# First weight unit in single k-tiles, a unit rounded ahead of the row scales, and two DVE instructions moved

## What is computed

```python
def rms_norm(x, g):
    y = x32 * lax.rsqrt(jnp.mean(x32 * x32, axis=-1, keepdims=True) + RMS_EPS)
    return (y * g).astype(x.dtype)

# layer 0: mla_stick_breaking_mixer (8 MLA heads, 8 stick-breaking heads), then swiglu
proj = u @ w_in            # u = rms_norm(x, g), 256 x 1024 by 1024 x 2208
h = h + (jax.nn.silu(u @ w_gate) * (u @ w_up)) @ w_down
# layer 1: chunk_band_mixer (16 heads, softmax over a band, p @ v, then w_out), then swiglu
s = softmax(q k^T * scale + bias); o = s @ v; h = h + o @ w_out
# last block: three attention branches (blocks, dilated, sliding window with a sink)
branches = [o_a * silu(ga), o_b * silu(gb), o_c * silu(gc)]
merged = sum(sigmoid(gate_logits) * (branches @ w_branch)); x = x + merged @ w_out
```

## Time and profile before

| | us |
|---|---|
| median of 3 runs | 980.27 (979.02 to 981.82) |
| the profiled execution | 978.15 |
| its span, first to last instruction | 976.4 |
| PE busy | 968.8 (99%), 4936 matmuls |
| DVE busy | 623.1 (64%) |
| ACT busy | 593.0 (61%) |
| POOL busy | 17.1 (2%) |

### The profile page before, as it was taken

How to read it: one execution, slowest core, us unless ns; L and a number is a source line. 1 busy time by engine, 2 the same in 40 slices (tenths; PEclk the granted TensorE clock), 3 DMA queues, 4 the chain that set the end, 5 groups by cost and what they waited for, 6 DMA issues and landing times.

```text
span 976.4 us, 13095 instructions
## 1 busy us (share of the span) xinstructions
PE 968.8 (99%) x4936; PEld 796.5 (82%) x4936; DVE 623.1 (64%) x765; ACT 593.0 (61%) x918; POOL 17.1 (2%) x30
## 2 busy tenths in 40 slices
PE   9999999999999999999999999999999999999998
PEld 7888788888888877788888888887878888788887
DVE  5776775555556767565555555867676667786654
ACT  6777665454445665464545445876767768857571
POOL 1000000000000000000000000000000000000000
PEclk9999999999999999999999999999999999999999
DMA  8536256756554553447666655565544443346551
GB/s 279 186 117 209 86 198 195 254 172 214 173 195 144 179 172 130 130 156 254 219 210 193 224 184 172 106 239 174 166 136 136 147 148 135 130 141 207 207 178 44
DMA packets 106078, 169.37 MB, mean 173 GB/s; under 512 B 4196, under 2 KB 65590, under 8 KB 106032
## 3 DMA queue, kind: packets, MB, share of 16 engines
q1 hardware_dynamic: 103392, 161.23, 50.5%
q0 software_dynamic: 2304, 7.40, 2.4%
q10 hardware_dynamic: 336, 0.10, 0.0%
HBM read 167.56 MB, written 1.16 MB: 173 GB/s over the span
## 4 chain that ended last, share of the span: by engine, by line
PE 97%; DVE 1%; DMA 1%; ACT 0%; issue 0%; SPq 0%; ACTq 0%
PE acc L519 14%; PE acc L521 14%; PE acc L520 14%; PE acc L577 12%; PE pair_ps L521 7%; PE pair_ps L519 7%; PE pair_ps L520 7%; PE acc L934 3%; PE acc L636 3%; PE turn_ps L725 2%; PE acc L754 1%; PE turn_ps L595 1%; PE pair_ps L708 1%; PE pair_ps L704 1%; PE turn_ps L519 1%; PE turn_ps L521 1%
## 5 line engine op out<-in xcount | busy, mean ns | idle before, releaser
L1992 DVE TENSOR_TENSOR w_lo<-w_raw,w_hi 128x2048 fp32r<-128x2048 f32 (+3 forms) x154 | 342.9, 2230 | 129.9 <-ACT w_hi L1252 129.6
L1252 ACT ACTIVATE w_hi<-w_raw 128x2048 fp32r<-128x2048 f32 (+3 forms) x154 | 286.4, 1863 | 87.4 <-PE acc L521 35.3
L519 PE MATMUL acc<-w_hi,uT_hi 128*128 128x512 f32 (+3 forms) x456 | 179.7, 394 | 2.3 <-DVE w_lo L1992 1.2
L521 PE MATMUL acc<-w_hi,uT_lo 128*128 128x512 f32 (+3 forms) x456 | 174.1, 382 | 0.0
L520 PE MATMUL acc<-w_lo,uT_hi 128*128 128x512 f32 (+3 forms) x456 | 173.8, 381 | 0.0
L519 PE MATMUL pair_ps<-w_hi,uT_hi 128*128 128x512 f32 x320 | 126.5, 395 | 0.0
L521 PE MATMUL pair_ps<-w_hi,uT_lo 128*128 128x512 f32 x320 | 124.9, 390 | 0.0
L520 PE MATMUL pair_ps<-w_lo,uT_hi 128*128 128x512 f32 x320 | 124.6, 389 | 0.0
L519 PEld LDWEIGHTS acc<-w_hi,uT_hi 128*128 128x128 f32 x456 | 85.7, 188 | 21.8 <-issue 4.2
L521 PEld LDWEIGHTS acc<-w_hi,uT_lo 128*128 128x128 f32 x456 | 85.6, 188 | 16.8
L520 PEld LDWEIGHTS acc<-w_lo,uT_hi 128*128 128x128 f32 x456 | 85.9, 188 | 14.3
(11 more groups left out here) (273 smaller groups left out, 1335.6 us busy)
## 6 DMA issues: line engine op xcount, KB each, us to landing
w_raw<-in_w_in SPq DMA_DIRECT2D x46, 1024.0 KB
w_raw<-in_w_gate SPq DMA_DIRECT2D x44, 512.0 KB
w_raw<-in_w_up SPq DMA_DIRECT2D x44, 512.0 KB
w_raw<-in_w_down SPq DMA_DIRECT2D x22, 1024.0 KB
w_raw<-in_w_out SPq DMA_DIRECT2D x12, 1024.0 KB
w_raw<-in_w_qkv SPq DMA_DIRECT2D x16, 512.0 KB
w_raw<-in_w_branch SPq DMA_DIRECT2D x6, 1024.0 KB
w_raw<-in_w_qkv SPq DMA_DIRECT2D x4, 1024.0 KB
```

What stands on the lines that cost most here:

```text
L519: mm(o, xh, wh[:, k, :], start=first and k == 0, stop=False)
L521: done = mm(o, xl, wh[:, k, :], start=False, stop=last and k == len(kts) - 1)
L1252: activation(w_hi[:, slot, 0:width], w_raw[:, slot, 0:width], ACT.Copy).then_inc(hi_done, 1)
L1992: v.tensor_tensor(w_lo[:, slot, 0:width], w_raw[:, slot, 0:width], w_hi[:, slot, 0:width].bitcast(f32), ALU.subtract).then_inc(lo_done, 1)
```

## The change

Four edits, in one file. The first unit's four k-tiles are handled one at a time on SP, ACT, DVE and PE; the input's first two k-tiles are also handled one at a time, in other PSUM banks (`input_banks`), and `keep_busy` behind the turns goes from 8 to 5. On ACT the rounding of unit 2 moves ahead of the g_col copies and of the wait for the row scales. In DVE's band mixer `probs(7)` moves one `slot_step()` up. In DVE's `gates_and_attend` one `slot_step()` moves from behind the two `maxima` to ahead of them.

```diff
+        input_banks = [(acc[2][:, :], 0, 1), (pair_banks[0], 1, 1), (pair_banks[1], 2, 2), (turn_banks[0], 4, 2),
+                       (turn_banks[1], 6, 2)]
...
-            def unit_in_halves(kt0):
+            def unit_in_parts(kt0, parts):
...
-            unit_in_halves(0)
-            unit_in_halves(4)
+            unit_in_parts(0, [(k, 1, (row_full + raw_full)[k]) for k in range(4)])
+            unit_in_parts(4, [(0, 2, second_full), (2, 2, raw_full[1])])
...
+                    for bank, kt0, m in input_banks:
+                        for k in range(m):
+                            done = transpose(bank[:, S * k + P * blk:S * k + P * blk + P],
+                                             h[:, blk, P * (kt0 + k):P * (kt0 + k) + P], ident[:, :])
...
-                keep_busy(8)
+                keep_busy(5)
...
-                unit_in_halves(0)
-                unit_in_halves(4, distances)
+                unit_in_parts(0, [(k, 1, first_lo, k + 1) for k in range(3)] + [(3, 1, lo_done, 1)])
+                unit_in_parts(4, [(0, 2, first_lo, 4), (2, 2, lo_done, 2)], distances)
...
                 scaled_by(MIX0)
                 slot_step(1536)
-                slot_step(1536)
                 copy = heads_copy(0)
...
             row_root(MIX0, D)
+            slot_step(1536)
             for group, row in enumerate((0, 2, 2, 2, 4)):
...
                 slot_step()
-                slot_step()
                 probs(7)
+                slot_step()
                 slot_step()
...
                 gate(1)
+                slot_step()
                 maxima(kind, 2, pair0, head0, bias_of)
                 maxima(kind, 3, pair0, head0, bias_of)
 
-                slot_step()
                 slot_step()
```

More of the change, by code:

```diff
@@ L212, in build_program @@
         gains_full = sem("gains_full")
-        first_full = sem("first_full")
+        row_full = [sem(f"row_full{i}") for i in range(3)]
         second_full = sem("second_full")
@@ L541, in chunk_unit, with unit_in_parts @@
                     n.chunk = n.chunk + 1
-            def unit_in_halves(kt0, between=None):
-                count = kt0 // 4 + 1
-                for k0, ready in ((0, first_lo), (2, lo_done)):
+            def unit_in_parts(kt0, split, between=None):
+                for k0, m, ready, count in split:
                     if between and k0:
@@ L549, in unit_in_halves @@
                     pe.wait_ge(ready, count)
-                    parts = [w[:, k0:k0 + 2, :] for w in unit_parts(4, 512)]
+                    parts = [w[:, k0:k0 + m, :] for w in unit_parts(4, 512)]
                     for blk in range(TB):
                         last = kt0 + k0 == 6
-                        done = half_unit(acc[blk][:, :], uT_hi, uT_lo, range(kt0 + k0, kt0 + k0 + 2), parts, blk,
+                        done = half_unit(acc[blk][:, :], uT_hi, uT_lo, range(kt0 + k0, kt0 + k0 + m), parts, blk,
                                          kt0 + k0 == 0, last)
@@ L661, in closing_unit @@
                 n.late = late
-                n.fresh = n.bank
+                n.fresh = {2 * i: n.bank + i + 1 for i in range(4)}
                 n.bank = n.bank + 4
@@ L2510, in swiglu, with part_of, input_part @@
                 n.handed, n.bank, n.exps = n0 + NF, b0 + NF, e0 + NF
-            def half_of(unit, half):
-                c = slice(1024 * half, 1024 * half + 1024)
-                dve.wait_ge(hi_done if half else first_hi, unit + 1)
+            def part_of(unit, k0, m, hi, count, lo):
+                c = slice(512 * k0, 512 * (k0 + m))
+                dve.wait_ge(hi, count)
                 v.tensor_tensor(w_lo[:, unit, c], w_raw[:, unit, c], w_hi[:, unit, c].bitcast(f32), ALU.subtract)\
-                    .then_inc(lo_done if half else first_lo, 1)
-            def input_pair(kt):
-                split_banks(uT_hi, uT_lo, kt, 2, stream_banks[MIX0][kt // 2:], MIX0)
+                    .then_inc(lo, 1)
+            def input_part(i):
+                bank, kt0, m = input_banks[i]
+                split_banks(uT_hi, uT_lo, kt0, m, [bank], MIX0)
             dve.wait_ge(gains_full, 32)
```

70 lines of the change are left out of this document (38 added, 32 removed).

## The result

| | before | after |
|---|---|---|
| median of 6 runs, us | 980.25 (978.3 to 981.82) | 974.88 (973.7 to 975.67) |
| the profiled execution, us | 978.15 | 975.67 |
| its span, us | 976.4 | 973.9 |

The ratio is 0.9945, with a 95% interval of 0.9931 to 0.996. The change takes 5.4 us off the median. The two profiled executions differ by only 2.5 us. So the median fell by more than the sum, and the profiled execution by less. Both have to be explained.

The account below looks back on a forecast made before the run. The prediction took PE, busy 99% of the span, to bound the kernel, with three waits to remove: 1.5 + 0.8 + 1.35 = 3.65 us, taking the median from 980.27 to 976.6 us, range 975.0 to 979.3.

Parts of the forecast that it names:

- the sum: Gains of the three places added: 1.5 + 0.8 + 1.35 = 3.65 us.
- place 1: First matmul: single k-tiles start PE at 8.95 instead of 10.52; 1.5 us kept after the step to the second chunk.
- the third unit: Step to the second chunk: unmoved rounding would hold PE 0.4 us on w_lo; moved, only 0.1 us on the accumulator copy.
- place 2: DVE's copy of prT at 402 us, moved ahead of a split, removes a PE wait: 0.8 us gained.
- place 3: DVE's split at 842 us, moved ahead of the maxima, removes a PE wait on w_lo: 1.35 us gained.
- Late maxima: Rival at place 3: ACT's longer chain holds PE at the second accumulator, half is lost; time 977.3; chance 0.10.
- the range: Range of the forecast time: 975.0 (upper ends 4.1, 1.2 scatter) to 979.3 (sum 1.85, 0.9 scatter).
- Slower queue: Rival at the start: twelve smaller transfers delay later loads; place 1 gives -0.3, time 978.4; chance 0.13.
- Later link: Rival: the start moves, a link behind it (fourth unit, accumulator copy) does not; place 1 lost, time 978.1; chance 0.12.
- the clock: Rival at PE's start: fewer fillers would mean a slower PE; the prediction gives no size; chance 0.05.

Follow-up runs that it names:

- after_pairs: The changed kernel with the row scales stored as 128 pieces of 8 bytes instead of 256 of 4, put in order by the load back: 973.52 us.
- start_pairs: The kernel before with the 8-byte store and only the edits at the start (single k-tiles, third unit, five fillers): 976.04 us.
- third_late: The changed kernel with the 8-byte store, but the rounding of the third unit back behind the g_col copies: 974.42 us.
- after_again: The changed kernel once more, unchanged, on another chip than the first measurement: 974.38 us.
- twice_in_turn: The kernel before with its store of the row scales made twice, the second when the first has landed: 985.2 us.
- busy8: The changed kernel with the 8-byte store and eight filler products instead of five ahead of the first product: 973.77 us.
- after_nostore: The changed kernel without the store of the row scales and the load back, scales filled with ones: 973.68 us.

## Why the prediction was right and wrong

**Right: what bounds the kernel, and place 1.** The forecast for the first product was 8.95, it came at 8.86. Some of that is luck: the chain started at 7.09 for the 7.16 reckoned, but in after it was PE's turn of the input that released it, not the gains, which were ready at 6.69; in after_pairs the same chain started at 6.60. The prediction had the third unit rounded from 16.9 to 18.4, the fourth by 20.3 and PE's step at about 21.05 with at most 0.1 us of wait; the trace has 16.91 to 18.38, 20.37 and 21.09 with none. The term was 1.5; the traces give 1.44, start_pairs 1.56. The piece prices read from neighbouring shapes (0.42, 0.65, 0.70) measured 0.47, 0.62 and 0.69.

**Right: places 2 and 3.** The waits went as forecast, and both gains are above their terms of 0.8 and 1.35. The traces give 0.97 and 1.50 at the places; alone the edits measured 1.18 and 1.50. The room behind place 3 came out as reckoned too. In before's time (0.98 us later than after's, there) the accumulator copy was to end at 846.4 and PE to take it at 846.8; the rows have 845.48 and 845.73, which are 846.46 and 846.71. Late maxima did not happen.

**Right with the wrong reason: the third unit.** The prediction said that without the move PE would be held 0.4 us, by w_lo. It is 0.7 to 0.9 by the medians, and last comes the copy of the accumulator (third_late). The move covers both, so the sum did not suffer.

**Wrong: the step from the sum to the median.** The step that failed reads: "The median of the runs was 980.27, 2.1 us above the profiled one, and the same gain gives 976.6." It takes the distance of 2.1 us for a constant that both kernels have. It is not. Without the stall before is at 977.5 to 977.6 and after at 973.5 to 973.8, on four chips. What lies above these floors differs from execution to execution and from one occasion to another: in before 2.7 us in the first median (980.25), then 1.5, 0.65 and 0.9; in after 1.3 in the first (974.88), then 0.7. The traces show what it is where it was traced, the wait at 643 behind the stall. The fall of 5.37 us is thus 3.8 to 4.1 from the change, and the other 1.3 to 1.5 is the difference between the two distances on the first occasion, 2.7 and 1.3. after_again shows that this part does not stay: on another chip the fall is 4.1. The terms of the sum were 0.2 to 0.4 too low, the one for place 2 most of all for its size (0.8 for 0.97). That is the small part of the miss, but without it the time would have been about 975.1 to 975.3, just inside the range.

**Wrong: the range.** It set 1.2 us of scatter under the upper ends of the terms, as if the scatter were the same noise for both. The three runs of before lay 2.8 us apart, and in a kernel that is bound by PE at 99% that asks for a cause. The trace of before had it: ACT's 3.06 us wait for a load of weights at 637.93, the longest of that kind in its list, with no wait of PE behind it. The prediction rests on PE's list and the three places of the change alone.

**The rivals.** Slower queue: falls for after, where ACT waits for no load in the first 20 us. It is not nothing in every execution: in start_pairs and third_late, with the same pieces, ACT waits 0.16 and 0.69 us for a load at 12.8 and 13.4 us; start_pairs still begins its second chunk at 20.75. Later link: the 1.5 us that the profiled execution gave back looks like it, but it lies at 643 us and before does the same without the change, so it falls as well. Late maxima and the clock: fall, as said.

**Open.** Why before's median lay 2.7 us above its floor on the first occasion and 0.65 to 1.5 on the others, and whether all of it was the stall. The traced executions show at most 1.5 us of wait from one store, so an extra 2.7 has been seen in no trace. Two things make the stall likely, without showing it. The store's landing varies (8.9 to 10.4 us for a first store, 13.3 for a second). And the two longest executions of before on the later occasions, 981.2 and 981.8 us, have a mean granted clock of 0.998, as those of twice_in_turn have (0.997 and 0.998), where all others of before show 0.999 or 1.0: PE seems to have stood so long in them that its clock fell for a while. Also open is why a store holds the loads up at all.

## What to carry to other kernels

Where a kernel's executions scatter by more than the engine that bounds it can explain, look for the cause before a gain is carried over to the median: list the waits for loads on the engines that feed it, and compare each with the room behind it. A wait that is just covered in one execution is a cost in the next (3.06 us for a room of 3.0 here, then 4.54). A small store in pieces of 4 bytes belongs away from a stream of loads, or it should go in larger pieces and be sorted on the way back.

## What the runs showed of the hardware

- A 1 KB store in 256 pieces of 4 bytes holds the loads of another queue below 100 GB/s, from about 400, for 8 to 9 us. Half as many pieces do so as long, 128 pieces of 8 bytes for 4 to 5 us, 128 of 64 bytes for less than 1, as no store at all.
- PE stood idle for 1.1 us at the start and kept its tempo; after a wait of 6.0 us behind 643 (twice_in_turn) its granted clock was 0.50 for the next 4 us, and 0.98 in the 4 us after that.
- The fillers behind the turns of the input started at 7.07, 7.59 and 7.71 us in three executions of kernels that are alike up to there (after_pairs, after, busy8), since the turns wait for the loads of x (after_nostore's list of waits has 0.5 us for them). Differences of this size at the start belong to no edit.
